# Gain rows spread by 128-row products, squares ahead of the gain copies, two recurrence copies on ScalarE, and a new instruction order, in a two-block token mixer

## The chip, the cores and the metric

The kernel runs on one core of a Trainium2 chip. The metric is the time on the device of one execution in microseconds: the median of three runs.

## What is computed

The reference is two transformer-like blocks, one behind the other, on 1024 tokens of width 1024, in float32. The first is cut here to what the change touches:

```python
def rms_norm(x, g):
    y = x * lax.rsqrt(jnp.mean(x * x, axis=-1, keepdims=True) + NORM_EPS)
    return y * g

h = rms_norm(x, pre_norm_w)
p = h @ w_in                       # 8320 columns: recurrence, convolution, pooling, gates
p_rwkv = token_shift(p_rwkv, mu)   # p + (p_prev - p) * mu
# per head (8 heads of 64), over 1024 tokens:
sa = state @ a_t
state = state * w_t + outer(sa, b_t) + outer(v_t, k_t)
y_t = state @ r_t
# group norm, bonus and gate; convolution and pooling branches; three gated
# branch projections; output projection; residual
```

The second block has windowed attention with sinks, a retention in both directions, and a feed-forward part of 2816 hidden channels whose last product is the down projection.

## The kernel before

All large products are float32 by parts: each operand is split into a high part, rounded for TensorE (`Whi`, `Hhi`), and the rest (`Wlo`, `Hlo`), and three products hi x hi, lo x hi and hi x lo are summed in PSUM (`dense`). ScalarE makes the high part, VectorE or GpSimd the low one. The first product is written in quarters of 256 tokens for its first two 128-column tiles, since the normed tokens are not all there yet.

**The start.** The tokens come in 8 tiles of 128 (`xs`, 5 buffers). ScalarE squares and sums each (`token_squares`, into `xj`), GpSimd raises the sum to -1/2 (`rstd`, `ss`), VectorE multiplies tile, factor and gain row (`token_norms`, into `xn`, 3 buffers), TensorE transposes 128x128 pieces into PSUM (`tokens_in`), ScalarE rounds them into `Hhi` and VectorE makes `Hlo`. The gain row is needed on all 128 partitions: TensorE multiplies a column of ones, 1x128, by the row, 1x512 twice, and ScalarE copies the result to `g_row` (`begin`). `xn0` holds the ones and `xn1` the row until the first norms. `WARM` counts the products of zeros that TensorE runs before and behind this.

**The recurrence.** The scan is cut into chunks of 64 tokens. A unit is two heads by 512 tokens, 8 units in all, 8 chunks each. Per unit `prep` makes decays and keys (`Cc`, `Ee`, `kkn`, `rk`, `kp`, `BK`), `invert` builds the chunk matrices (`AB`) and inverts them on VectorE by 60 small steps (`Nn`, `Ntmp`), `stage` turns them into the chunk operators (`WU`, `Zt`), and `chain` carries the state `Xs` from chunk to chunk: a product on TensorE, a multiply on VectorE, 64 times. All of it is woven into the stream of dense products of the first projection (`kb`, `rb`, `RAV` are its results for keys, r and v). Two steps matter here: the copies of the transposed values from PSUM into `WU` rows 64 to 127 (VectorE, in `stage`, two per unit; ScalarE copies rows 0 to 63), and the transposition of the inverse inside SBUF into `Nt` (VectorE, last step of `invert`; the trace calls both `Nn`), which SP then writes out (`scr_xt`).

**The down projection.** A Strassen-like scheme with 7 block products (`PRODUCTS["w"]`). Its weights come as `wSrcA..`, VectorE sums them to `wSrcS..`, ScalarE rounds to `wHi..`, VectorE or GpSimd make `wLo..`; the hidden values (`hT..`, `hB..`) go the same way, and the results are summed in `acc`.

**What sets the order.** Each engine's program is a set of streams (generators), one letter each, and `weave` takes steps from them in the order of a string per engine in `ORDER`. The engines run strictly in that order, and synchronize by semaphores alone. `PICKS` says which PSUM bank each use takes. In `ORDER["pe"]` d is a dense step (two 512-column products), a a token transposition, p, i, s, c and g are the recurrence's streams; in `ORDER["act"]` Z is `begin`, q the squares, a the rounding of tokens, w the weight rounding.

The helpers record all operations at one line each: products L120, transposes L123, ScalarE L126, VectorE's and GpSimd's two-operand operations L129, scalar ones L133 and L134, with a tensor L137, copies L140, memsets L143, transfers L146.

## Time and profile before

| | |
|---|---|
| runs | 2243.98, 2244.04, 2244.3 us; median 2244.04 |
| the profiled execution | 2244.64 us |
| its span, first to last instruction | 2242.9 us |
| busy: PE, VectorE (DVE), ScalarE (ACT), GpSimd (POOL) | 99%, 69%, 37%, 21% |
| mean granted clock of TensorE | 0.998 |

A share of busy time is read against the span. The busy time of PE includes products that run at a lower clock, and a product's record is longer than the time to the next one's start, since products are pipelined: how fast they run is read from the distance of their starts. A row's idle time stands in brackets with what ended it.

### The profile page before, as it was taken

Reading aid. Unit: us, or ns where it says so; the run is one execution under the profiler, and the core shown is the slowest. Engines: PE = TensorE matmul, PEld = TensorE weight load, DVE = VectorE, ACT = ScalarE, POOL = GpSimd, SP = SyncE. Lnnn points to the kernel's source line nnn. Section 1 sums busy time; section 2 is a strip of 40 time slices with the busy share of each in tenths; the row PEclk is TensorE's granted clock in tenths of the full one; section 3 lists DMA queues with packets and bytes.
Section 4 is the critical chain, followed back from the end, with each engine's and each line's share of the span. In section 5 each row is a group of like instructions: output and inputs, shape, how many; then the busy total and the mean of one; then the engine's idle time right before and its main releaser. Section 6 shows DMA issues by size and latency. Waiting matters only on the chain.

```text
span 2242.9 us, 30930 instructions
## 1 busy us (share of the span) xinstructions
PE 2218.5 (99%) x11960; PEld 1835.1 (82%) x11960; DVE 1554.3 (69%) x2646; ACT 837.8 (37%) x1486; POOL 476.1 (21%) x379
## 2 busy tenths in 40 slices
PE   9999999999999999999999999999999999999998
PEld 7778788777788888888888888888888888887777
DVE  6775886778858444665448777754776666678998
ACT  5334243333444334223334454542333333345441
POOL 2000000000002321143122212200122222236552
PEclk9999999999999999999999999999999999999999
DMA  4122221221233334853221212133222222233334
GB/s 151 44 57 53 64 58 35 62 56 58 65 113 116 113 113 150 291 169 129 91 72 52 59 38 59 39 127 113 76 85 85 85 78 82 85 115 106 107 122 149
DMA packets 254547, 208.55 MB, mean 93 GB/s; under 512 B 49985, under 2 KB 223681, under 8 KB 254402
## 3 DMA queue, kind: packets, MB, share of 16 engines
q1 hardware_dynamic: 254400, 206.58, 29.6%
q8 instruction: 95, 1.56, 0.3%
q14 instruction: 50, 0.41, 0.1%
q10 hardware_dynamic: 2, 0.00, 0.0%
HBM read 151.48 MB, written 47.71 MB: 89 GB/s over the span
## 4 chain that ended last, share of the span: by engine, by line
PE 79%; DVE 14%; issue 2%; DMA 2%; SPq 1%; POOL 1%; ACT 1%; DVEq 0%; POOLq 0%; ACTq 0%
PE PS L120 77%; PE PS L123 3%; DVE Nn L129 2%; DVE Ntmp L129 2%; SPq L146 1%; DVE Wlo L129 1%; DMA Nn<-scr_ns 1%; DVE acc L129 1%; DMA wSrcA<-in_w_down_dram 1%; DVE wSrcS L129 1%; DVE Zt L129 1%; DVE cy L137 1%; DVE ST L137 1%; POOL wLoA L129 0%; DVE Xs L129 0%
## 5 line engine op out<-in xcount | busy, mean ns | idle before, releaser
L120 PE MATMUL PS<-Hhi,Wlo 128*128 128x512 f32 (+1 forms) x1304 | 421.4, 390 | 0.0
L120 PE MATMUL PS<-Hlo,Whi 128*128 128x512 f32 (+1 forms) x1304 | 420.5, 389 | 0.0
L120 PE MATMUL PS<-Hhi,Whi 128*128 128x512 f32 (+1 forms) x1304 | 419.5, 388 | 0.9 <-DVE Hlo L129 0.9
L120 PEld LDWEIGHTS PS<-Hhi,Whi 128*128 128x128 f32 x1304 | 240.3, 189 | 45.9 <-issue 2.0
L120 PEld LDWEIGHTS PS<-Hhi,Wlo 128*128 128x128 f32 x1304 | 239.1, 189 | 45.9 <-issue 2.4
L120 PEld LDWEIGHTS PS<-Hlo,Whi 128*128 128x128 f32 x1304 | 239.6, 189 | 44.9 <-issue 2.2
L126 ACT ACTIVATE Whi<-Wraw 128x512 fp32r<-128x512 f32 x170 | 106.4, 629 | 333.7 <-PE PS L120 333.3
L129 DVE TENSOR_TENSOR Wlo<-Wraw,Whi 128x512 fp32r<-128x512 f32 x166 | 121.4, 734 | 73.2 <-ACT Whi L126 72.4
L129 DVE TENSOR_TENSOR Ntmp<-Nn 32x30 f32<-32x30 f32 (+14 forms) x240 | 76.7, 319 | 23.3 <-DMA Nn<-scr_ns 17.1
L129 POOL TENSOR_TENSOR sm<-sm,expo 128x8 f32<-128x8 f32 x8 | 17.3, 2165 | 340.4 <-DVE sm L134 340.3
L129 DVE TENSOR_TENSOR Nn<-Nn,Ntmp 32x30 f32<-32x30 f32 (+14 forms) x240 | 76.6, 319 | 6.9
L129 DVE TENSOR_TENSOR acc<-PS,acc 128x512 f32<-128x512 f32 x108 | 71.0, 679 | 10.4 <-PE PS L120 10.2
L129 POOL TENSOR_TENSOR Wlo<-wA,Whi 128x512 fp32r<-128x512 f32 x38 | 51.0, 1342 | 110.6 <-ACT Whi L126 110.6
L129 DVE TENSOR_TENSOR wS<-wA,wA 128x512 f32<-128x512 f32 x38 | 26.1, 688 | 57.9 <-DMA wA<-in_w_gate_dram 57.9
L120 PE MATMUL PS<-YMlo,Whi 128*128 128x512 f32 (+1 forms) x188 | 64.7, 372 | 0.0
L120 PE MATMUL PS<-YMhi,Whi 128*128 128x512 f32 (+1 forms) x188 | 64.6, 371 | 0.0
L120 PE MATMUL PS<-YMhi,Wlo 128*128 128x512 f32 (+1 forms) x188 | 64.5, 371 | 0.0
L126 ACT ACTIVATE smx<-smx,small,q_norms 128x385 f32<-128x385 f32 (+1 forms) x64 | 43.1, 675 | 47.7 <-DVE small L137 47.7
L129 POOL TENSOR_TENSOR rsb<-rsb,expo 128x8 f32<-128x8 f32 x8 | 13.2, 1654 | 218.3 <-DVE rsb L133 218.3
L120 PE MATMUL PS<-YMhi,fSlo 128*128 128x512 f32 x152 | 59.1, 389 | 0.0
L120 PE MATMUL PS<-YMlo,fShi 128*128 128x512 f32 x152 | 59.1, 389 | 0.0
L120 PE MATMUL PS<-YMhi,fShi 128*128 128x512 f32 x152 | 59.1, 389 | 0.0
(497 smaller groups left out, 5216.8 us busy)
## 6 DMA issues: line engine op xcount, KB each, us to landing
Wraw<-in_w_in_dram SPq DMA_DIRECT2D x126, 256.0 KB, 2.9
scr_g<-stg SPq DMA_DIRECT2D x24, 512.0 KB, 3.1
tg<-scr_g SPq DMA_DIRECT2D x24, 512.0 KB, 4.3
scr_fb<-fb SPq DMA_DIRECT2D x22, 512.0 KB, 4.1
gwA<-in_w_in_dram SPq DMA_DIRECT2D x40, 256.0 KB, 3.4
wA<-in_w_gate_dram SPq DMA_DIRECT2D x38, 256.0 KB, 3.2
wA<-in_w_up_dram SPq DMA_DIRECT2D x38, 256.0 KB, 3.3
wSrcA<-in_w_down_dram SPq DMA_DIRECT2D x48, 192.0 KB, 2.9
```

What stands on the lines that cost most here:

```text
L120: return self.h.matmul(out, lhsT, rhs, start=start, stop=stop, skip_group_check=True)
L123: return self.h.transpose(out, in_, ident)
L126: return self.h.activation(out, in_, func, **kw)
L129: return self.h.tensor_tensor(out, a, b, op)
L137: return self.h.scalar_tensor_tensor(out, a, s, b, op0, op1)
L146: return self.h.dma_start(out, in_)
```

## The change

Six things change.

1. The gain row is spread by products with 128 rows: `xn2` columns 0 to 127 are zero but for row 0, which is 32, and `xn1` is zero but for row 0, the gains. VectorE fills `xn2`, GpSimd fills all of `xn1` first, and the transfer of the row, on ScalarE's queue, waits for that. The factor 32 was in ScalarE's copy before.
2. `WARM` goes from (4, 8) to (5, 2).
3. ScalarE squares the first three token tiles ahead of the gain copies, which now wait for the norm of tile 1.
4. VectorE norms tiles 0 and 1 with the gains read from PSUM, and from tile 2 on with `g_row`.
5. ScalarE copies both halves of `WU` and makes the `Nt` transposition.
6. All five order strings and the bank picks are new.

```diff
--- before.py
+++ after.py
@@ -17,7 +17,7 @@
 ORDER2 = ("aq", "rk", "rv", "rq")
 NXS, NXN = 5, 3
 NRAW, NSPL = 3, 4
-WARM = (4, 8)
+WARM = (5, 2)
 KAPPA = float(np.exp(-0.5))
 EPS = 1e-6
 GN_EPS = 64 * 1e-5
@@ -659,11 +659,11 @@
         pe.wait_ge(*S.start_dve.at("zero"))
         for i in range(WARM[0]):
             pe.mm(SB[3], K.Whi[NSPL - 1][:, 0, :], K.Whi[NSPL - 1][:])
+        pe.wait_ge(*S.start_dve.at("one"))
         pe.wait_ge(*S.grow_dma.at(0))
         for j in range(2):
-            bank, _ = banks.take(("gain", j), (f"SB{j}",), [S.init_act.at("gain")])
-            t = pe.mm(bank, K.xn[0][0:1, 0:128], K.xn[1][0:1, j * 512:j * 512 + 512])
-        t.then_inc(*S.xtr_pe.tick("gain"))
+            bank, _ = banks.take(("gain", j), (f"SB{j}",), [S.init_act.at("gain"), S.xn_dve.at((1, j))])
+            pe.mm(bank, K.xn[2][:, 0:128], K.xn[1][:, j * 512:j * 512 + 512]).then_inc(*S.xtr_pe.tick(("gain", j)))
         for i in range(WARM[1]):
             t = pe.mm(SB[3], K.Whi[NSPL - 1][:, 0, :], K.Whi[NSPL - 1][:])
         t.then_inc(*S.xtr_pe.tick("warm"))
@@ -949,7 +949,7 @@
             cb = hf * 8
             na = K.NA[u % 2]
             for g in range(2):
-                bk, before = banks.take(("av", u, g), SIDE, [S.stage_act.at(("a", u, g)), S.stage_dve.at(("v", u, g))])
+                bk, before = banks.take(("av", u, g), SIDE, [S.stage_act.at(("a", u, g))])
                 for m in before:
                     pe.wait_ge(*m)
                 pe.wait_ge(*S.prep_dve.at(("r", u)))
@@ -977,7 +977,7 @@
             for m in before:
                 pe.wait_ge(*m)
             pe.wait_ge(*S.inv_dve.at(("A", u, 1, 1)))
-            pe.wait_ge(*S.stage_dve.at(("v", u, 1)))
+            pe.wait_ge(*S.stage_act.at(("a", u, 1)))
             for c in range(8):
                 for h in range(2):
                     t = pe.mm(bk[64 * h:64 * h + 64, c * 64:(c + 1) * 64], na[64:128, h, c, :], K.WU[64:128, h, c, 64:128])
@@ -1253,11 +1253,13 @@
         return (S.w_raw0, S.w_raw1, S.w_raw2)[n % NRAW].at(n)
 
     def begin():
+        act.wait_ge(*S.xrstd_pool.at("row"))
         act.dma(K.xn[1][0:1, :], K.D["pre_norm_w"]).then_inc(*S.grow_dma.tick(0, by=16))
         yield
-        act.wait_ge(*S.xtr_pe.at("gain"))
+        act.wait_ge(*S.xtr_pe.at(("gain", 1)))
+        act.wait_ge(*S.xn_dve.at((1, 1)))
         for j in range(2):
-            act.act(K.g_row[:, j * 512:j * 512 + 512], banks.of(("gain", j)), ACT.Copy, scale=32.0).then_inc(*S.init_act.tick("gain"))
+            act.act(K.g_row[:, j * 512:j * 512 + 512], banks.of(("gain", j)), ACT.Copy).then_inc(*S.init_act.tick("gain"))
         yield
 
     def weights():
@@ -1411,12 +1413,18 @@
                 src = banks.of(("av", u, g)).rearrange("p (c h f) -> p h c f", c=4, h=2)
                 act.wait_ge(*S.stage_pe.at(("av", u, g)))
                 act.wait_ge(*S.init_dve.at("wu"))
-                act.act(K.WU[0:64, :, 4 * g:4 * g + 4, 0:64], src[0:64], ACT.Copy).then_inc(*S.stage_act.tick(("a", u, g)))
+                act.act(K.WU[0:64, :, 4 * g:4 * g + 4, 0:64], src[0:64], ACT.Copy).then_inc(*S.stage_act.tick())
+                act.act(K.WU[64:128, :, 4 * g:4 * g + 4, 64:128], src[64:128], ACT.Copy).then_inc(*S.stage_act.tick(("a", u, g)))
                 yield
                 src = banks.of(("bk", u, g)).rearrange("p (c h f) -> p h c f", c=4, h=2)
                 act.wait_ge(*S.stage_pe.at(("bk", u, g)))
                 act.act(K.BKT[:, :, 4 * g:4 * g + 4, :], src, ACT.Copy).then_inc(*S.stage_act.tick(("bk", u, g)))
                 yield
+            act.wait_ge(*S.inv_dve.at(("dg", u)))
+            if u:
+                act.wait_ge(*S.xtw_dma.at(u - 1))
+            act.act(K.Nt, K.Nn[0:16].rearrange("p s t -> p t s"), ACT.Copy).then_inc(*S.stage_act.tick(("nt", u)))
+            yield
             act.wait_ge(*S.stage_pe.at(("m1", u)))
             act.wait_ge(*S.init_dve.at("v1"))
             for a in range(0, 128, 32):
@@ -1823,9 +1831,11 @@
     omu, bones, maskA, rst = K.omu, K.c_("bones"), K.c_("maskA"), K.c_("rst")
 
     def begin():
-        dve.memset(K.xn[0][0:1, 0:128], 1.0).then_inc(*S.start_dve.tick("one"))
         dve.memset(K.xse[:, :, 1024:1025], float(np.sqrt(1024 * EPS))).then_inc(*S.start_dve.tick("eps"))
         dve.memset(K.Whi[NSPL - 1][:].bitcast(F32), 0.0).then_inc(*S.start_dve.tick("zero"))
+        dve.memset(K.xn[2][:, 0:128], 0.0).then_inc(*S.start_dve.tick("rows"))
+        dve.wait_ge(*S.start_dve.at("rows"))
+        dve.memset(K.xn[2][0:1, 0:128], 32.0).then_inc(*S.start_dve.tick("one"))
         dve.memset(K.expo[:], -0.5).then_inc(*S.start_dve.tick("expo"))
         yield
 
@@ -1839,13 +1849,17 @@
                 yield
 
     def token_norms():
-        dve.wait_ge(*S.init_act.at("gain"))
         for i in range(8):
+            if i == 2:
+                dve.wait_ge(*S.init_act.at("gain"))
             if i >= NXN:
                 dve.wait_ge(*S.xtr_pe.at((i - NXN, 1)))
             dve.wait_ge(*S.xrstd_pool.at(i))
             for cols, keys in ((slice(0, 512), [(i, 0)]), (slice(512, 1024), [(i, 1), i])) if i < 2 else ((slice(0, 1024), [(i, 0), (i, 1), i]),):
-                dve.stt(K.xn[i % NXN][:, cols], K.xs[i % NXS][:, cols], K.ss[:, 8 + i:9 + i], K.g_row[:, cols], ALU.mult,
+                gain = banks.of(("gain", keys[0][1])) if i < 2 else K.g_row[:]
+                if i < 2:
+                    dve.wait_ge(*S.xtr_pe.at(("gain", keys[0][1])))
+                dve.stt(K.xn[i % NXN][:, cols], K.xs[i % NXS][:, cols], K.ss[:, 8 + i:9 + i], gain, ALU.mult,
                         ALU.mult).then_inc(*S.xn_dve.tick(*keys))
                 yield
 
@@ -2057,11 +2071,6 @@
             dve.wait_ge(*S.inv_dve.last())
             dve.ts(dg, dg, 1.0, ALU.add).then_inc(*S.inv_dve.tick(("dg", u)))
             yield
-            if u:
-                dve.wait_ge(*S.xtw_dma.at(u - 1))
-            dve.wait_ge(*S.inv_dve.last())
-            dve.cp(K.Nt, Nn[0:16].rearrange("p s t -> p t s")).then_inc(*S.inv_dve.tick(("nt", u)))
-            yield
 
     def stage():
         for u, (p, hf) in enumerate(UNITS):
@@ -2072,13 +2081,6 @@
             dve.cp(EC[:, 0, :], K.Ee[0:64, :, 64]).then_inc(*S.stage_dve.tick())
             dve.cp(EC[:, 1, :], K.Ee[64:128, :, 64]).then_inc(*S.stage_dve.tick(("EC", u)))
             yield
-            for g in range(2):
-                src = banks.of(("av", u, g)).rearrange("p (c h f) -> p h c f", c=4, h=2)
-                dve.wait_ge(*S.stage_pe.at(("av", u, g)))
-                if u:
-                    dve.wait_ge(*S.stage_pe.at(("de", u - 1, 1, 1)))
-                dve.cp(K.WU[64:128, :, 4 * g:4 * g + 4, 64:128], src[64:128]).then_inc(*S.stage_dve.tick(("v", u, g)))
-                yield
             for g in range(2):
                 for h in range(2):
                     b3 = banks.of(("de", u, g, h))[0:64, :].rearrange("p (i j x f) -> p i j x f", i=2, j=2, x=2)
@@ -2680,6 +2682,8 @@
         pool.tt(out, out, K.expo[:, 0:out.shape[1]], ALU.pow).then_inc(*sig.tick(key))
 
     def token_norms():
+        pool.memset(K.xn[1][:], 0.0).then_inc(*S.xrstd_pool.tick("row"))
+        yield
         for i in range(8):
             pool.wait_ge(*S.start_dve.at("expo"))
             pool.wait_ge(*S.xsq_act.at(i))
@@ -2869,7 +2873,7 @@
             sp.wait_ge(*S.inv_dve.at(("dg", u)))
             sp.dma(D["scr_xs"][u], K.Nn.rearrange("p s t -> p (s t)")).then_inc(*S.xsw_dma.tick(u, by=16))
             yield
-            sp.wait_ge(*S.inv_dve.at(("nt", u)))
+            sp.wait_ge(*S.stage_act.at(("nt", u)))
             sp.dma(D["scr_xt"][u], K.Nt.rearrange("p s t -> p (s t)")).then_inc(*S.xtw_dma.tick(u, by=16))
             yield
             xs_v = D["scr_xs"][u].rearrange("(b q) (s t) -> b s q t", b=2, s=32)
@@ -3164,68 +3168,68 @@
 
 ORDER = {
     "pe":
-        "a5d24a2d14a2d36a2d7a2d27a2d10a2d78pd5pd8pd18id3pd20id7s2d5s2d4pd5pd9pd19id41pd5id7s2d4sd7s2d5s2d5scs"
...
+        "a4d18a3d17a2d22a2d8a2d20a2d10ad2ad99pd4pd8pd20id3pd19sdsd3s2d5id4pd4pd8pd16id61pd4id9s2d4sd5s2d3s2d3"
...
```

Three places of the order. First ScalarE at the start of the program, as a piece of the difference (`xj` are the squares, `g_row` the gain copies; - before, + now):

```order
-L126 ACTIVATE g_row<-PS 128x512 x2
 L126 ACTIVATE xj,ss<-xs 128x1025 x2
-L126 ACTIVATE Hhi<-PS 128x4x128
 L126 ACTIVATE Whi_55<-Wraw_52 128x512
-L126 ACTIVATE Whi_56<-Wraw_53 128x512
-L126 ACTIVATE Hhi<-PS 128x4x128
 L126 ACTIVATE xj,ss<-xs 128x1025
 L126 ACTIVATE Hhi<-PS 128x4x128
+L126 ACTIVATE Whi_56<-Wraw_53 128x512
+L126 ACTIVATE Hhi<-PS 128x4x128
+L126 ACTIVATE g_row<-PS 128x512 x2
 L126 ACTIVATE xj,ss<-xs 128x1025
```

The gain copies moved from the first place to behind the third square and the second `Hhi`; the second `Whi` moved behind the first `Hhi`.

Second, VectorE at the end of the fourth inversion and the shift of the third `kb`, before:

```order
L133 TENSOR_SCALAR Nn<-Nn 32x32
L2132 TENSOR_REDUCE sm<-Yy 128x8
L129 TENSOR_TENSOR Wlo_62<-Wraw_53,Whi_58 128x512
L134 TENSOR_SCALAR sm<-sm 128x8
L140 COPY Nn<-Nn 16x1024
L137 SCALAR_TENSOR_TENSOR kb<-PS,par,kb 128x1023
```

and now:

```order
L133 TENSOR_SCALAR Nn<-Nn 32x32
L129 TENSOR_TENSOR Yy<-Yy,BV_92 128x512
L129 TENSOR_TENSOR Wlo_62<-Wraw_53,Whi_58 128x512
L137 SCALAR_TENSOR_TENSOR kb<-PS,par,kb 128x1023
```

The first row ends the inversion. The transposition is gone from between it and `kb`. On ScalarE, at the same place, now (`rk` is the square of `kb` that TensorE waits for):

```order
L126 ACTIVATE Nn_95<-Nn_95 16x1024
L126 ACTIVATE Whi3_58<-Wraw1_53 128x512
L126 ACTIVATE kb_81<-PS,drv_65 128x1024
L126 ACTIVATE rk_89<-kb_81,par_64 128x512
```

where before the rows were the same without the first.

Third, ScalarE in the down projection, between the third and the fourth weight block of 384 columns, before:

```order
L126 ACTIVATE hB21hi3_318<-hB21raw3_320 128x512
L126 ACTIVATE acc10_356<-PS 128x512
L126 ACTIVATE acc12_358<-PS 128x512
L126 ACTIVATE wHiS3_326<-wSrcS3_344 128x384
L126 ACTIVATE acc19_365<-PS 128x512
L126 ACTIVATE hT4hi3_321<-hT21_281 128x512
L126 ACTIVATE acc18_364<-PS 128x512
L126 ACTIVATE hB11hi0_236<-hB11raw0_238 128x512
L126 ACTIVATE wHiS4_328<-wSrcS4_345 128x384
```

and now:

```order
L126 ACTIVATE hB21hi3_318<-hB21raw3_320 128x512
L126 ACTIVATE acc10_356<-PS 128x512
L126 ACTIVATE wHiS3_326<-wSrcS3_344 128x384
L126 ACTIVATE acc12_358<-PS 128x512
L126 ACTIVATE acc19_365<-PS 128x512
L126 ACTIVATE wHiS4_328<-wSrcS4_345 128x384
```

`hT4hi3`, `acc18` and `hB11hi0` moved behind the weights.

## Rows read from the trace of the kernel before

**Rows 1.** The page: busy time, share of the span and instructions of each engine.

```profile
PE 2218.5 (99%) x11960; PEld 1835.1 (82%) x11960; DVE 1554.3 (69%) x2646; ACT 837.8 (37%) x1486; POOL 476.1 (21%) x379
```

**Rows 2.** Who waited for whom, PE: total us, times, longest.

```profile
PE PS L120 <- DVE Xs L129: 2.5, 6, 0.7
PE PS L120 <- ACT rk L126: 2.2, 3, 1.1
PE PS L120 <- ACT wHiS L126: 2.1, 2, 1.9
PE PS L120 <- DVE wLoS L129: 2.0, 5, 0.6
```

**Rows 3.** Windows: stretch, length, PE, PEld, DVE, ACT, POOL busy, granted clock, DMA, GB/s.

```profile
324.50:327.90 3.40, 3.40 (x9) 2.63 (x8) 0.05 (x1) 0.35 (x1) 2.25 (x2) 0.50 0.48 106
2051.70:2055.10 3.40, 3.40 (x10) 2.64 (x9) 1.44 (x2) 1.31 (x4) 3.27 (x3) 0.50 0.23 66
```

**Rows 4.** Timeline, 2048 to 2056: start us, duration us, engine, operation [idle before, releaser].

```profile
2048.99 0.60 ACT L126 ACTIVATE acc<-PS 128x512 f32<-128x512 f32 x1 [0.74 <-PE PS L120]
2049.62 0.63 ACT L126 ACTIVATE hB11hi<-hB11raw 128x512 fp32r<-128x512 f32 x1
...
2048.09 1.53 DVE L129 TENSOR_TENSOR wSrcS<-wSrcA,wSrcS 128x384 f32<-128x384 f32 x1
...
2050.80 0.47 PE L120 MATMUL PS<-hB22hi,wHiS 128*128 128x512 f32 x1 [1.85 <-ACT wHiS L126]
...
2052.46 0.63 PE L120 MATMUL PS<-hB22hi,wLoS 128*128 128x512 f32 x1
2052.89 0.63 PE L120 MATMUL PS<-hB22hi,wHiS 128*128 128x512 f32 x1
...
2055.53 0.40 PE L120 MATMUL PS<-hT2lo,wHiS 128*128 128x512 f32 x1
2055.76 0.39 PE L120 MATMUL PS<-hT2hi,wLoS 128*128 128x512 f32 x1
```

**Rows 5.** Timeline of the start, and the landing times of the token tiles (tile xs).

```profile
3.58 3.78 PE L120 MATMUL PS<-xn,xn 1*128 1x512 f32 x4
...
7.29 3.58 PE L120 MATMUL PS<-Whi 128*128 128x512 f32 x8
7.39 1.08 ACT L126 ACTIVATE g_row<-PS 128x512 f32<-128x512 f32 x2 [4.85 <-PE PS L120]
8.36 1.06 ACT L126 ACTIVATE xj<-xs 128x1025 f32<-128x1025 f32 x1
...
11.25 0.63 PE L123 MATMUL PS<-cst,xn 128*128 128x128 f32 x4 [0.38 <-DVE xn L137]
...
14.91 0.36 PE L120 MATMUL PS<-Hhi,Whi 128*128 128x256 f32 x1 [0.89 <-DVE Hlo L129]
...
18.80 0.36 PE L120 MATMUL PS<-Hhi,Whi 128*128 128x256 f32 x1
...
DMA to landing us min/median/max: 3.6/5.8/8.0
```

**Rows 6.** Groups by line and form, GpSimd's copies and VectorE's largest memset: busy, mean ns.

```profile
L140 POOL COPY kp<-rsb 128x512 f32<-128x512 f32 x8 | 5.6, 696 | 0.4
...
L143 DVE MEMSET WU<- 64x1024 f32 x1 | 0.9, 912 | 0.3 <-issue 0.3
```

**Rows 7.** Timeline, 321.9 to 323.

```profile
321.99 0.72 ACT L126 ACTIVATE rk<-kb,par 128x512 f32<-128x512 f32 x1 [2.45 <-DVE kb L137]
...
322.86 1.02 PE L120 MATMUL PS<-cst,rk 128*128 128x2 f32 x8 [1.06 <-ACT rk L126]
```

**Rows 8.** Groups by line and form, the copies that move, and ScalarE's into WU.

```profile
L140 DVE COPY WU<-PS 64x512 f32<-64x512 f32 x16 | 11.1, 694 | 5.2 <-PE PS L123 4.8
L140 DVE COPY Nn<-Nn 16x1024 f32<-16x1024 f32 x8 | 8.9, 1107 | 0.7
...
L126 ACT ACTIVATE WU<-PS 64x512 f32<-64x512 f32 x64 | 37.9, 592 | 34.1 <-PE PS L120 17.3 <-PE PS L123 15.9
```

More of the change, by code:

```diff
@@ L3227 @@
[L3227 to L3228 removed]
+    "2320101320132013200101011010010101011010011001010101010101001010110100101111010101010100101011010011"
+    "0101010101001010101101010110101011010101001101010010101101010101010010101010110100101111010101010100"
+    "1010010110101010100100101010101010101101010010101011067423501674235016742350167423501674235016742350"
@@ new lines @@
+    "1671010101010101010101010102102010110101001201101010120012011012012012012001201201201102102201200120"
+    "1021012101201210210210200120120120112012012010201021101201201021022120120002012012011201201200120120"
+    "1201210121021020120120102012010210211021021021012012010201021101201201012001011010120100110120101245"
+    "0123674501236745012367450123674501236745012367450123674501236745012367450123674501236745012360174560"
+    "1237456012374560123745602137456021374560213745602137456021374123012134231022137502201020321"
```

102 lines of the change are left out of this document (47 added, 55 removed).

## The prediction, made before the change ran

> **What bounds the kernel now.** I read the engine shares first, then who waited for whom on TensorE, then the timeline at the longest waits. [rows 1]: PE is busy 2218.5 us of the 2242.9 us span, every other engine 69% or less. So a change can gain only what PE loses: idle time, or time on a slow clock. Idle is 2242.9 - 2218.5 = 24.4 us, 1.1% of the span. [rows 2] names it: PE waited 2.5 us for Xs (the recurrence's state), 2.2 us for rk, 2.1 us for wHiS, 2.0 us for wLoS, and less for the rest. The second loss is not in the busy time. In two stretches of 3.4 us the granted clock was 0.50 [rows 3], that is 1.2 instead of 2.4 GHz. In the second of them 512-column products follow each other every 0.43 us, right behind it every 0.23 us [rows 4]: 3.41/0.43 = 8 products where 15 would fit, so one such stretch costs (0.43 - 0.23) x 8 = 1.6 us. Both come right behind a wait of PE: 1.06 us for rk at 322.9 [rows 7], 1.85 us for wHiS at 2050.8 [rows 4].
>
> The profiled execution took 2244.64 us (span 2242.9), 0.6 us over the median 2244.04. The sum is made against 2244.64, and 0.6 comes off at the end.
>
> **The start: -2.0 us.** Before, ScalarE has nothing to do until the gains are spread. PE runs 4 warm products, waits for the row, runs the four records of the 1-row products in 3.78 us and the 8 warm products in 3.58 us, 0.45 each, near the 0.43 of [rows 4] at half the clock: this was 1.2 GHz too. ScalarE copies the gains at 7.39 (1.08 us) and only then squares, from 8.36, though the first token tile landed 3.6 us after its issue at 0.72, at 4.3 [rows 5]. The first transposes run at 11.25 and the first dense product at 14.91 [rows 5].
>
> What now happens, step by step. (1) GpSimd fills xn1, 128x1024, before the row's transfer may start. The trace has no such fill. Bounds: 0 us and 1.4 us, two of its 128x512 copies of 0.70 [rows 6]; VectorE's 64x1024 memset took 0.91 [rows 6], nearest in shape, and GpSimd is the slower of the two elsewhere, so I take 1.1. The row then leaves at about 1.9 instead of 0.71. It landed at most 2.9 us after its issue (3.58 - 0.71); now it goes beside the token tiles, so I take 3.1: it lands at 5.0. (2) PE: 5 warm products end at 1.6 + 5 x 0.43 = 3.7, PE waits 1.3 us, the gain products take 3.4 us (four records, 0.85 apart) to 8.4, two warm products to 9.3. The first transposes come at 9.3 instead of 11.25. (3) ScalarE squares tiles 0 and 1 from 4.3, 1.06 and a 0.2 us read each, to 6.9, and is free of the gains. Its next square waits for tile 2, which leaves SP ahead of one 256 KB weight piece now: median landing 5.8 us behind issue at 3.87 was 9.7, now some 0.8 earlier, 8.8. Then square 2 to 10.0, Hhi 0.60, Whi 0.62, Hhi 0.60 to 11.9; Hlo on VectorE 0.69 and hand-overs 0.3: first dense product at 12.9, 2.0 earlier. (4) VectorE reads the gains of tiles 0 and 1 from PSUM: its copies out of PSUM took 0.69 us for 512 columns [rows 8], no more than the 0.75 of this product from SBUF, so I count 0. (5) The second half of the contraction needed Hlo of (1,1), and began at 18.80. Now behind 11.9: gain copies 1.1, square 1.25, Hhi 0.6, Whi 0.6, Hhi 0.6, Hlo 0.9 = 17.0. Again about -2.0. The later tiles are then fed by ScalarE, which began its squares 4 us earlier, so nothing should take the 2 us back. Bounds: -3.4 (the row lands unhindered, the clock rises during the gain products, which saves half of their 3.4 us) and +1.7 (below). Five warm products fewer are inside this count.
>
> **The recurrence copies: -1.2 us.** Per unit VectorE loses two WU copies, 2 x 0.694, and the Nn transposition, 1.107: 2.5 us, over 8 units 20 us. ScalarE takes the first two at 2 x 0.592 [rows 8] and the third at about what VectorE needed: 2.3 us per unit, 18 us. It has room (37% busy, [rows 1]), and PE does not wait for either engine's total. What counts is the 2.5 + 2.2 = 4.7 us that PE waited for Xs and rk, both behind VectorE [rows 2]. Only one of these waits shows a moved copy in its chain, the one at 322.9: rk waited 2.45 us for kb, and PE then 1.06 us for rk [rows 7]; the Nn copy stood right ahead of kb on VectorE (the second place of the order). Now ScalarE has the Nn copy ahead of its own kb copy, with one Whi between them, where before it made the kb copy while VectorE transposed. Counted from the end of the inversion the chain to rk gets no shorter, so this wait goes only if the inversion ends earlier. It may: VectorE has 2.5 us less to do per unit. I take a quarter of the 4.7 us, -1.2. Bounds: all of it, -4.7, and as much again, +4.7, since every step of the order moved and each new place can be late. The slow stretch at 324.5 I leave in: 0, with bounds of -1.6 and, for a third one, +1.6.
>
> **The new order in the down projection: -3.3 us.** At 2048.6 PE waits 1.85 us for wHiS. The operand wSrcS is computed by 2049.6, but ScalarE works in order and has an acc copy that waits 0.74 us for PE, and hB11hi, ahead of wHiS [rows 4]. The third place of the order shows this wHiS right behind acc19, and on VectorE its source now stands ahead of hT1lo and hT, two subtractions that stood ahead of it. With hB11hi (started 0.5 us before wHiS could) and the late acc out of the way, and the source two 512-column subtractions of 0.6 to 0.7 us earlier, 1.7 of the 1.85 us go, and with the wait the slow stretch behind it, 1.6 us. Bounds: 0 (another operand is as late) and -3.5. The shorter wLoS waits, 2.0 us in five [rows 2], stay: 0. The last 30 rows of PE stand as before: 0.
>
> **Sum**: 2244.64 - 2.0 - 1.2 - 3.3 = 2238.1; less 0.6 is 2237.5 us, -0.3%.
>
> **A rule against the change.** The first 256-column dense products, from 14.91, ran 0.12 us apart, the pace of 2.4 GHz, although 16 transposes were all that PE did in the 3.6 us ahead of them. The Trainium skill (TensorE: Matmul & The Clock Gate, Part 4) says that a transpose does not count as busy time for the clock the way a product does, and Part 1 that the clock is slow until PE has been kept busy. By that rule the wait for the row and two warm products instead of eight leave the clock low at 12.9. What it would cost is rival C; the trace so far speaks for the clock staying up, since the same transposes did it no harm.
>
> **The rivals.**
> A (forecast), 2237.5: start, copies and the down projection as above. For it: each of the three has a row. Chance 0.50, its own range 2234 to 2241.
> B, the order gives it back: the start gains 2.0, but new waits and a new slow stretch take the place of the old ones, as nearly every row moved and the old order too left 24.4 us idle. 2244.0 - 2.0 + (0 to 2) = about 2242.5. Chance 0.25.
> C, the slow clock at the first dense products: PE idles 1.3 us in the middle of its warm-up, and the clock is still at 1.2 GHz, or falls to it, for one stretch like those of [rows 3] from 12.9 on. That costs 1.6 us, and the rest comes as in A: 2239.1. Against it: before, 3.58 us of warm products went ahead of the transposes; now 3.4 + 0.9 = 4.3 us of 128-row products do. Chance 0.08.
> D, slower: ScalarE reaches the Nn transposition before the inversion ends and stands there, with the weight conversions (Whi) of the dense stream behind it. VectorE cannot make Wlo, and PE starves. One converted piece feeds PE for 24 products of 0.23 = 5.5 us, so this begins to cost when ScalarE stands longer than that; 1.3 us over it per unit is 8 x 1.3 = 10.4, less the 5.3 of the start and the down projection: 2244.0 + 5.1 = 2249.1. Against it: ScalarE is idle 63% of the span, so it can run several pieces ahead. Chance 0.08.
> E, more goes: the slow stretch at 324.5 too, and all but 1.2 of the 4.7 us for Xs and rk: 2237.5 - 1.6 - 2.3 = 2233.6. Chance 0.09.
>
> **How the numbers follow.** A measurement tells 0.2%, 4.5 us, from no change: the borders are 2239.6 and 2248.5. Faster: 0.42 of A's 0.50, E's 0.09, 0.05 of C, 0.02 of B: 0.58. Slower: D beyond the border, 0.07. Same: 0.35. The range leaves out D and the lower part of E: 2232.5 to 2244.5.
>
> **What would show it.** In the new profile: the first square at about 4.3, first transposes near 9.3, first dense product near 12.9 at 0.12 us spacing. Spacing 0.21 there means C. No wait for wHiS at 2046 and clock 1.00 around it. PE's waits for Xs and rk under 4.7 us in sum. Nn on ScalarE with idle time before it, followed by PE waits for Whi or Wlo, would mean D. The prediction is wrong if PE's idle time is 24 us again, or if the slow stretches are two or more.

## The result, and the profile after

| | before | after |
|---|---|---|
| median of the runs timed together, us | 2244.16 (20 runs) | 2247.93 (20 runs) |
| ratio, 95% interval | | 1.0018, 1.0011 to 1.0025 |
| profiled execution, us | 2244.64 | 2249.11 |
| its span, us | 2242.9 | 2247.0 |

The changed kernel is slower by 3.8 us, a difference just inside the 0.2% that I called no change and well outside my range (2232.5 to 2244.5). It was forecast faster by 6.5 us. Both signs that I had named for a wrong prediction are there: PE's idle time is over 24 us, and the slow stretches are two.

First the groups that answer to [rows 1] and [rows 2], of the changed kernel: the page's shares, then who waited for whom on PE.

```profile
PE 2217.8 (99%) x11955; PEld 1834.4 (82%) x11955; DVE 1534.7 (68%) x2623; ACT 864.8 (38%) x1510; POOL 487.0 (22%) x380
```

```profile
PE PS L120 <- DVE wLoS L129: 3.7, 7, 1.6
PE PS L120 <- ACT wHiS L126: 3.5, 3, 1.4
PE PS L123 <- DVE smx L133: 2.5, 2, 2.0
PE PS L120 <- DMA xn<-in_pre_norm_w_dram: 1.5, 1, 1.5
```

PE is as busy as before and idles 29.2 us instead of 24.4. Xs and rk have left the head of the list; wLoS and wHiS have grown from 4.1 to 7.2 us, and a wait for smx is new.

To see where, I cut both spans at the same dense products. The windows of the kernel before are the start, the recurrence, the plain stretch, attention with retention, the feed-forward, and the down projection with the end (columns as in [rows 3]):

```profile
0.00:14.90 14.90, 11.45 (x32) 6.53 (x33) 4.72 (x10) 7.54 (x13) 3.21 (x8) 1.00 0.59 198
14.90:715.90 701.00, 692.36 (x4104) 569.76 (x4104) 536.83 (x1089) 262.45 (x463) 54.52 (x38) 1.00 0.24 67
715.90:1171.00 455.10, 454.32 (x2105) 379.25 (x2104) 235.81 (x265) 154.76 (x240) 114.91 (x87) 1.00 0.43 142
1171.00:1515.00 344.00, 342.89 (x2473) 287.30 (x2472) 256.08 (x582) 166.46 (x326) 74.20 (x58) 1.00 0.22 63
1515.00:2020.00 505.00, 504.21 (x2302) 419.73 (x2301) 322.20 (x395) 159.43 (x268) 120.34 (x104) 1.00 0.28 90
2020.00:2242.90 222.90, 213.30 (x951) 172.54 (x949) 198.70 (x306) 87.12 (x179) 108.94 (x85) 0.98 0.39 119
```

and those of the changed kernel:

```profile
0.00:13.80 13.80, 9.28 (x24) 5.30 (x24) 4.97 (x11) 7.58 (x13) 5.07 (x10) 1.00 0.85 293
13.80:707.90 694.10, 689.99 (x4107) 569.46 (x4108) 510.27 (x1065) 289.99 (x486) 59.55 (x37) 1.00 0.24 67
707.90:1163.10 455.20, 454.42 (x2106) 379.15 (x2105) 236.02 (x266) 154.72 (x240) 116.09 (x88) 1.00 0.43 142
1163.10:1513.40 350.30, 345.84 (x2473) 288.41 (x2472) 254.07 (x581) 166.06 (x326) 75.72 (x58) 1.00 0.22 61
1513.40:2018.40 505.00, 504.22 (x2302) 419.75 (x2301) 320.98 (x396) 159.74 (x269) 123.42 (x104) 1.00 0.28 90
2018.40:2247.00 228.60, 214.09 (x951) 172.35 (x949) 208.38 (x305) 86.73 (x179) 107.12 (x86) 0.98 0.38 117
```

The first number behind each stretch is its length. Start -1.1 us, recurrence -6.9, attention +6.3, down projection with the end +5.7; the other two stretches are equal to 0.1 us. In the two stages whose code it edits the change gains 8 us, where I had 3.2. It loses 12 us in two stages where it alters nothing but the order and the choice of PSUM banks.

These shares come from one trace of each kernel. Seven of the traces below, this one and those of runs 1, 3, 4, 8, 10 and 11, share the changed start, copies and order of the recurrence; at the plain stretch they lead the trace of the kernel before by 5.3 to 9.5 us, this one by 7.9. So a stage's figure from one pair of traces may be off by some 2 us, and the ratios of whole runs carry the argument.

The slow clock moved too. In the changed kernel the granted clock is 0.50 from 1195.7 and from 2066.1:

```profile
1195.70:1199.10 3.40, 3.40 (x10) 2.64 (x9) 3.27 (x8) 0.56 (x1) 0.15 (x1) 0.50 0.20 52
2066.10:2069.50 3.40, 2.96 (x7) 2.39 (x8) 3.07 (x3) 0.73 (x2) 3.40 (x3) 0.50 0.04 11
```

The stretch at 324.5 [rows 3] is gone, one in the attention has come, and in the down projection the place is 2066.1 instead of 2051.7. The first begins 1.5 us behind the end of PE's longest wait of its stage, 2.02 us for smx at 1194.2. The second begins at 2066.1, inside the longest wait of its stage, 1.55 us for wLoS, which ends at 2066.5; the wait before that one, 1.42 us for wHiS, ends at 2064.3.

### The profile page after: what moved, and what is told of

The parts are those of the page before. It is cut to its first block, busy times and chain, and to the rows that moved or that the text cites. A ratio compares the mean times of both kernels' runs of the same rounds, so it can differ in the third digit from the quotient of the medians.

```text
span 2247.0 us, 30905 instructions
## 1 busy us (share of the span) xinstructions
PE 2217.8 (99%) x11955; PEld 1834.4 (82%) x11955; DVE 1534.7 (68%) x2623; ACT 864.8 (38%) x1510; POOL 487.0 (22%) x380
## 4 chain that ended last, share of the span: by engine, by line
PE 80%; DVE 13%; DMA 2%; issue 2%; ACT 1%; POOL 1%; SPq 1%; DVEq 0%; ACTq 0%; POOLq 0%
PE PS L120 77%; PE PS L123 3%; DVE Ntmp L129 2%; DVE Nn L129 2%; DMA wSrcA<-in_w_down_dram 1%; DVE wSrcS L129 1%; DVE ST L137 1%; SPq L146 1%; DVE acc L129 1%; DVE Wlo L129 1%; DVE wLoS L129 1%; DVE Zt L129 0%; DVE Xs L129 0%; DVE hT L129 0%; POOL wLoA L129 0%
## 5 line engine op out<-in xcount | busy, mean ns | idle before, releaser
L126 ACT ACTIVATE WU<-PS 64x512 f32<-64x512 f32 x80 | 47.4, 593 | 36.5 <-PE PS L123 18.0
L129 POOL TENSOR_TENSOR wLoA<-wSrcA,wHiA 128x384 fp32r<-128x384 f32 (+1 forms) x48 | 54.1, 1145 | 11.9 <-ACT wHiA L126 11.9
```

The source lines that it names most:

```text
L126: return self.h.activation(out, in_, func, **kw)
L129: return self.h.tensor_tensor(out, a, b, op)
```

## The experiments

All ratios are against the kernel before, timed in alternation with each; 0.001 is 2.2 us. The recurrence and the attention are separated by a plain stretch that takes the same time in both traces (455.1 and 455.2 us), and so are the attention and the down projection by the feed-forward (505.0 in both). In the middle of these one order can be cut off and the other set on.

**1 to 4. Which stage loses?** Each kernel takes the order and the banks of each stage from one of the two kernels.

```diff
 ORDER, PICKS              recurrence   attention   down projection
 early_new                 changed     -changed     -changed
                                       +before      +before
 late_new                 -changed      changed      changed
                          +before
 down_old                  changed      changed     -changed
                                                    +before
 attention_old             changed     -changed      changed
                                       +before
```

The start goes with the recurrence.

> The changed kernel up to the middle of the plain stretch of dense products after the recurrence (all edits of the code, its order of the start and the recurrence), and from there on the order and banks of the kernel before. Theory 1 (each stage keeps what its own order gives: start and recurrence -7.9 us, attention and retention +6.3, down projection +5.0, read at the same dense products of the two traces): about 7.9 us under the kernel before, 2236.3, a ratio of 0.9965. Theory 2 (the later losses come from the earlier part being 8 us early, by another timing of transfers and of the clock, whatever the order of the later stages): the loss is here too, 2244 to 2248. Theory 3 (the gain up to the middle is real, but any change of timing costs a slow stretch of the clock or two): 2238 to 2241.

> The reverse: the kernel before with its own code and order up to the same place, and from there on the changed kernel's order and banks (attention, retention, feed-forward, down projection). Theory 1: +6.3 and +5.0, about 2255.5, a ratio of 1.005. Theory 2: no loss, 2243 to 2246. Theory 3: 2246 to 2250.

> The changed kernel with the order and banks of the kernel before from the middle of the feed-forward stretch on, so in the down projection alone. Theory 1: the changed kernel less 5.0 us, 2242.6, 1.6 us under the kernel before. Theory 2: as the changed kernel, 2247 to 2248, since what comes ahead is the same. In the trace the waits of TensorE for wHiS and wLoS near 2062 us should be gone by theory 1.

> The changed kernel with the order and banks of the kernel before in the attention and retention stage alone (from the middle of the plain stretch to the middle of the feed-forward). Theory 1: the changed kernel less 6.3 us, 2241.3, and no wait of 2 us for smx near 1192 us nor the slow clock behind it. Theory 2: 2247 to 2248.

| | ratio, 95% | theory 1 |
|---|---|---|
| early_new | 0.9966, 0.9953 to 0.9978 | 0.9965 |
| late_new | 1.0056, 1.0043 to 1.0068 | 1.005 |
| down_old | 0.9986, 0.9977 to 0.9995 | 0.9993 |
| attention_old | 0.9995, 0.9986 to 1.0004 | 0.9987 |

Theory 1 holds in all four, theory 2 in none. Every order carries its gain or loss with it, whichever half stands ahead: 0.9966 and 1.0056 leave +0.0022 together, and the change measured +0.0018. So the later stages do not lose because they begin 8 us earlier; they lose because of how their own steps stand. Order and PSUM banks were always exchanged together here, so the four runs don't tell one from the other. Theory 3, slow stretches brought by any change of timing, was the rival in runs 1 and 2. It is not in the medians, but the one trace of run 1 has two slow stretches, from 14.2 and from 1423.9.

**5. The start alone.** The changed start, and everything behind it as before.

> The kernel before with the changed start alone (row products with 128 rows, memsets, warming products 5 and 2, first two tiles normed from PSUM, and the order of the first 13 us); everything behind the first few dense products, the recurrence's copies too, as before. My sum had -2.0 us; the trace of the changed kernel has the first dense product only 1.1 us earlier. Theory 1 (the stages add up): 1.1 us under the kernel before, ratio 0.9995. Theory 2 (an early shift is used up by the next wait for data): no change, 1.000.

Measured 0.9987, 0.9978 to 0.9996: 2.9 us, more than either theory. In its trace the first dense product is 1.3 us earlier, and the lead grows to 1.7 us by 297 us and to 2.9 by 368 us. Between these two lies 324.5, where the kernel before had its slow stretch and this run had none. Theory 2 is refuted. The slow stretch is missing in run 9 too, whose start is the old one and whose wait for rk at 321.7 is longer (1.49 us against 1.06), so its absence does not need the changed start; 1.3 us is what this trace gives to the start itself.

**6 and 9. The copies with the old order.** Before's order and start, with the 16 WU copies and the 8 Nn copies on ScalarE. First the Nn copy stood right before the step that reads m1:

```diff
 ScalarE, each unit
     bk(1)
-    m1
+    Nt <- Nn
+    m1
```

> The kernel before with its own order and start, but with the copies of the recurrence moved: the 16 copies into the second half of WU and the 8 transposing copies of Nn run on ScalarE, each at the place in ScalarE's order where its result is next read there (the Nn copy right before the step that reads m1). Theory A (the copies themselves bring the recurrence's gain, by taking some 20 us of work off VectorE): most of the 6.8 us, 2238 to 2240. Theory B (they bring it only together with the new order, which uses the freed time): within 1.5 us of the kernel before, 2242.5 to 2245. Theory C (my rival D: ScalarE stands at the Nn copy before the inversion ends, and its queue is late for what TensorE reads): slower, 2247 or more.

It took 2321.08 us, 1.0342: slower as in theory C, and far beyond it, but by another way, since ScalarE never stood at the copy; it came to it late. The waits of PE in its trace:

```profile
PE PS L120 <- DMA X11t<-scr_xt: 54.7, 8, 9.4
```

The copy goes to DRAM and comes back transposed before PE can use it. Counted from the copy's begin on ScalarE to the step on m1 this took 8.6 to 9.9 us in each of the eight units. The inversion ended at 346.8 in the fourth unit, and ScalarE began the copy only at 359.5. The 54.7 us are not the whole of the 77. The stretch of the recurrence, which ran from 14.9 to 715.9 in the kernel before, is now

```profile
15.00:793.00 778.00, 718.76 (x4103) 592.41 (x4104) 517.29 (x1066) 289.56 (x487) 53.51 (x38) 0.94 0.21 61
```

PE idles 59.2 us in it instead of 8.6, and is busy 26.4 us longer with the same products, since the granted clock is 0.50 in eight stretches of it, 95.6 us in all; seven of them are 10 to 20 us long. So the place is what failed, and I put it where ScalarE stood in the trace of before when the inversion ended:

```diff
 ScalarE, each unit
     bk(1)
+    Nt <- Nn
     (2 to 9 steps of other streams)
-    Nt <- Nn
     m1
```

(The 32 places and the 4 us in the text below are slips of mine: it is 2 to 9 places, and the copies had begun 6.2 to 14.4 us behind the inversion's end.)

> As the run with the copies alone, but the eight transposing copies of Nn stand in ScalarE's order where, in the trace of the kernel before, the inversion ends (ScalarE's next instruction there starts 0.3 us or more after VectorE's step on the diagonal), 2 to 32 places ahead of where they stood. In that run each began 4 to 15 us after the inversion's end, and TensorE waited 54.7 us for X11t, the transfer behind it. Theory C' (only the place of the Nn copy cost it): those waits go, and the time is within 3 us of the kernel before, 2241 to 2247. Theory C'' (ScalarE is late all through the recurrence with 20 us more work in this order): still over 2255.

Measured 0.9991, 0.9982 to 1.0000: theory C'. The same instructions on the same engine cost 77 us or gain 2, the latter at the edge of the interval, by the place of eight of the 24 copies alone. The wait for X11t is gone from its list; the one for Xs is down to 0.8, but rk now costs more than in [rows 2]:

```profile
PE PS L120 <- ACT rk L126: 2.9, 3, 1.5
...
PE PS L120 <- DVE AB L129: 1.8, 2, 1.2
```

**7 and 13. The recurrence without the start; its order without the copies.**

> The start of the kernel before, then the changed kernel's copies and its order of the recurrence, then the order of the kernel before from the middle of the plain stretch on. Theory 1: the 6.8 us that the traces show between the first dense product and 700 us, 2237.3, a ratio of 0.997; with the start alone it must add up to the -7.9 of the kernel with both. Theory 2 (start and recurrence work on one another): only -4 or less.

Measured 0.9968, 0.9956 to 0.9981: theory 1. The two parts add up to -0.0045 by their ratios, where the kernel with both has -0.0034; the intervals allow that. Then the copies went back to VectorE, in the new order:

```diff
 VectorE, each unit
     EC
+    WU[64:128] <- av(0)      (where ScalarE's copy began)
+    WU[64:128] <- av(1)
 ...
     Nn diagonal
+    Nt <- Nn
```

> The changed start and the changed order of the recurrence, but the copies on VectorE as in the kernel before: each WU copy stands in VectorE's order where ScalarE's began in the changed kernel's trace, the Nn copy right behind the inversion; from the middle of the plain stretch on as before. With the copies too this kernel was at a ratio of 0.9966, and with the start alone at 0.9987, so order and copies together bring 0.0021, some 5 us. Theory K (the copies bring it, the order only follows): 0.9985 to 0.999, as with the start alone. Theory L (the order brings it, whoever copies): 0.9966 to 0.9972. Theory M (this order has no room for 20 us more of VectorE): above 1.000.

Measured 1.0012, 1.0003 to 1.0021: theory M. The waits of PE in its trace:

```profile
PE PS L120 <- DVE Xs L129: 6.9, 15, 0.8
PE PS L120 <- DVE AB L129: 3.4, 4, 1.3
```

against these of the kernel with copies and order (the seventh run):

```profile
PE PS L120 <- DVE RAV L129: 1.5, 3, 0.7
...
PE PS L120 <- DVE Xs L129: 1.0, 4, 0.4
```

With the start's share (0.9987) taken off, the recurrence reads: copies with the old order -0.0009, order without the copies +0.0025, both -0.0021 to -0.0032. Neither part brings the gain by itself as it was tried. That the new order has no room for 20 us more on VectorE is my reading and is not shown: the copies stood at one set of places only, and runs 6 and 9 show how much a place can do.

**8. Two steps exchanged in the attention.** At 1191 PE stands for smx. All engines of the changed kernel there:

```profile
1191.12 0.49 DVE L137 SCALAR_TENSOR_TENSOR ST<-ST,small,PS 64x64 f32<-64x64 f32 x2
...
1191.51 2.35 POOL L129 TENSOR_TENSOR ro<-ro,sinT 128x1024 f32<-128x1024 f32 x1 [20.85 <-DMA ro<-qr]
...
1191.65 2.43 DVE L133 TENSOR_SCALAR smx<-smx,small 128x384 f32<-128x384 f32 x1
1194.11 0.49 DVE L137 SCALAR_TENSOR_TENSOR ST<-ST,small 64x64 f32<-64x64 f32 x2
...
1194.22 0.85 PE L123 MATMUL PS<-cst,smx 128*128 128x128 f32 x6 [2.02 <-DVE smx L133]
```

VectorE's scaling took 2.43 us; the median of this instruction is 0.41. It began 0.14 us behind GpSimd's product and ended 0.22 us behind its end. The exchange puts it 0.49 us earlier:

```diff
 VectorE
     small <- 1/small
+    smx <- smx*small
     ST <- ST*small+PS  (2)
-    smx <- smx*small
     ST <- ST*small     (2)
```

> The changed kernel with two neighbouring steps of VectorE exchanged, near 1191 us: the scaling of smx that TensorE waits 2.0 us for now stands ahead of two additions into ST that nobody waits for. In the changed kernel it began at 1191.65, 0.14 us behind GpSimd's product of 128x1024 (1191.51 to 1193.86), and ended at 1194.08, 2.43 us for what takes 0.41 elsewhere. Theory P (a VectorE operation with two operands or such a scaling stands while GpSimd's runs, so the place decides who pays): smx takes 0.4 us, TensorE's wait of 2.18 us goes, the slow clock of 3.4 us at half speed behind it (1.6 us) goes too, and the additions into ST take 2.4 us instead: 3.5 us under the changed kernel, 2244.2. Theory Q (the wait is for something else that is late, and only moves): less than 1 us.

The trace of that kernel:

```profile
1192.57 0.42 DVE L133 TENSOR_SCALAR smx<-smx,small 128x384 f32<-128x384 f32 x1
...
1193.15 2.39 POOL L129 TENSOR_TENSOR ro<-ro,sinT 128x1024 f32<-128x1024 f32 x1 [22.06 <-DMA ro<-qr]
1193.43 2.40 DVE L137 SCALAR_TENSOR_TENSOR ST<-ST,small 64x64 f32<-64x64 f32 x2
1193.57 0.88 PE L123 MATMUL PS<-cst,smx 128*128 128x128 f32 x6
```

and, as a window, the time in which the slow stretch had been:

```profile
1193.80:1200.00 6.20, 6.20 (x39) 5.04 (x39) 6.07 (x8) 1.12 (x2) 1.74 (x1) 1.00 0.07 17
```

Theory P in each point: smx takes 0.42 us, the two additions into ST take 2.40 instead of 0.49, PE doesn't wait, and the clock stays at 1.00. Across this place the trace gains 3.3 us on the changed kernel's. The ratio is 1.0005 (0.9996 to 1.0014) where the changed kernel had 1.0018 (1.0011 to 1.0025), 2.9 us less, and the two intervals overlap a little. The kernel before meets the same GpSimd product with additions into ST, which nobody reads soon.

Of these 3.3 us the wait is the exchange's, and the slow stretch may be chance. Runs 2, 3 and 10 have the old place of smx and waits of 2.1, 1.9 and 1.7 us for it; a slow stretch follows in run 3 alone. Against run 10, which had the wait and no slow stretch, the exchange gains 1.3 us at this place.

Not every instruction of VectorE stands. One that reads PSUM ran at its usual 0.55 us inside another such product of the changed kernel:

```profile
1365.98 2.39 POOL L129 TENSOR_TENSOR rot<-rot,sinT 128x1024 f32<-128x1024 f32 x1 [0.47 <-DMA rot<-ro]
...
1366.13 0.55 DVE L2319 CUSTOM_DVE_ANT_0 smx<-PS,cse 128x384 f32<-128x384 f32 x1
```

And where VectorE began first, at 1234.06 with a product of 128x1024 that took its usual 1.23 us, GpSimd's, begun at 1234.11, took 3.44 us instead of 2.39. The Trainium skill (SBUF — State Buffer, "SBUF: two separate sides") says that the two engines share a pair of ports, and that the instruction that starts first holds it to its end while the other stands; it says so of VectorE's instructions with two SBUF inputs, against a GpSimd instruction that reads SBUF, and of those in a two-port mode, not of all. The trace agrees: 2.43 us against 0.41 where GpSimd was first, 3.44 against 2.39 where VectorE was, and 0.55 as ever for the one that reads PSUM.

**10. One window of the down projection.** The first long waits there, in the changed kernel:

```profile
2062.37 0.68 DVE L129 TENSOR_TENSOR hT<-hB21raw,hT 128x512 f32<-128x512 f32 x1
2062.98 0.55 DVE L129 TENSOR_TENSOR wSrcS<-wSrcA,wSrcS 128x384 f32<-128x384 f32 x1
2063.09 0.63 ACT L126 ACTIVATE hT4hi<-hT 128x512 fp32r<-128x512 f32 x1 [2.76 <-DVE hT L129]
...
2063.63 1.33 ACT L126 ACTIVATE wHiS<-wSrcS 128x384 fp32r<-128x384 f32 x3
...
2065.13 2.63 DVE L129 TENSOR_TENSOR wLoS<-wSrcS,wHiS 128x384 fp32r<-128x384 f32 x2
```

```profile
2064.28 0.47 PE L120 MATMUL PS<-hB22hi,wHiS 128*128 128x512 f32 x1 [1.42 <-ACT wHiS L126]
...
2066.54 0.79 PE L120 MATMUL PS<-hB22hi,wLoS 128*128 128x512 f32 x1 [1.55 <-DVE wLoS L129]
```

On VectorE the source of S4's wHiS (the second row) stands behind hT and an acc addition, both of which it led in the old order. ScalarE stands 2.76 us at hT4hi with the three wHiS behind it. The edit gives this one window of 16 the old order:

```diff
 VectorE, fifth window            ScalarE, fifth window
-  hT3lo S3 hT2lo hT1lo loS3       -  ... B21hi hiS3 hT4hi hiS4 hiS2 hiS1 hiA12 hiA22
-  S1 acc S2 hT S4 acc             +  ... hiS3 acc acc B21hi hiS4 hiS2 hiS1 hiA12 hiA22 hT4hi
-  hT4lo loS4 loS2
+  S3 acc hT3lo loS3 S1 hT2lo S2
+  hT1lo S4 hT acc loS4 loS2
+  acc hT4lo
```

> The changed kernel with one of the 16 windows of the down projection (the fifth, 2054 to 2066 us) in the order of the kernel before: 18 steps of VectorE and 14 of ScalarE, so the sums S1, S2 and S4 stand ahead of two low halves and one addition into acc, and ScalarE's wHi copies ahead of hT4hi, for which it stood 2.76 us. Theory 1 (that order is what TensorE's waits of 1.59 and 1.72 us at 2062 and 2065 are from): they shrink to some 1.2 us together as in the run with the old down projection, and the slow clock at 2066.1 (1.6 us) goes; at most 2.1 + 1.6 us, so 2244 to 2246 against 2247.9. Theory 2 (the next window, in its new order, then waits for what this one did not): less than 1 us, 2247 to 2248.

Measured 1.0007, 0.9998 to 1.0016, 2.5 us under the changed kernel, whose interval (1.0011 to 1.0025) overlaps this one. The longest waits for wHiS and wLoS only fall from 1.42 and 1.55 to 1.0 and 1.1 us. The rest is the clock: this trace has no slow stretch in the down projection before its end. From 2020 us to the last dense product it gains 2.1 us on the changed kernel's, of the 5 that the whole stage lost. But runs 2 and 4 have this window in the new order with the same two waits, 1.4 and 1.6 us, and no slow stretch behind them either. So some 0.8 us of waits belong to this window; that the slow stretch does is not shown, and theory 2 is unlikely rather than refuted. The other windows were not tried one by one.

**11. The best of both in the down projection.** The changed order for its first four windows, where the trace had gained 3.0 us, and the old one behind.

> The changed start and recurrence; attention and retention as before; of the down projection the first four windows in the changed order and the rest as before. By the traces the changed order gains 3.0 us up to the fifth window (2061 against 2020 us) and loses 8 behind it. Theory 1: 3.0 under the kernel with all of the later order as before (ratio 0.9966), 2233, a ratio of 0.9953. Theory 2 (the wait of 2.2 us only moves to the fifth window): 2235.6 as without.

Measured 0.9971, 0.9959 to 0.9982: theory 2. The wait for wHiS, 2.05 us before 2046.0 in the trace of run 1, is gone, and three of 1.35, 0.74 and 1.09 us end at 2030.5, 2059.7 and 2061.5, with a slow stretch from 2062.1. It brings nothing over 0.9966 that could be told. The gain of my third term is given back within two windows.

**12 and 14. One row instead of 128.** The start waits for the row of norm weights. In the changed kernel:

```profile
0.71 0.95 POOL L143 MEMSET xn<- 128x1024 f32 x1 [0.29 <-POOLq L3318]
1.70 0.51 ACTq L146 DMA_DIRECT2D xn<-in_pre_norm_w_dram  x1
5.52 3.75 PE L120 MATMUL PS<-xn,xn 128*128 128x512 f32 x4 [1.55 <-DMA xn<-in_pre_norm_w_dram]
9.92 1.71 PE L123 MATMUL PS<-cst,xn 128*128 128x128 f32 x8
10.03 1.06 ACT L126 ACTIVATE xj<-xs 128x1025 f32<-128x1025 f32 x1 [0.73 <-DMA xs<-in_x_dram]
13.79 0.36 PE L120 MATMUL PS<-Hhi,Whi 128*128 128x256 f32 x1 [0.69 <-DVE Hlo L129]
```

```diff
-    pool.memset(K.xn[1][:], 0.0)
-    act.wait_ge(*S.xrstd_pool.at("row"))
-    dve.memset(K.xn[2][:, 0:128], 0.0)
-    pe.mm(bank, K.xn[2][:, 0:128], K.xn[1][:, j * 512:j * 512 + 512])
+    pe.mm(bank, K.xn[2][0:1, 0:128], K.xn[1][0:1, j * 512:j * 512 + 512])
```

> The kernel with the best of both orders, but with row products of one row as in the kernel before (no clearing of xn by GpSimd and VectorE, and the transfer of the norm weights does not wait for it), still read from PSUM and ahead of the copies. In the changed kernel the transfer is issued at 1.70 us, behind GpSimd's memset (0.71 to 1.66), TensorE stands 1.55 us for it and the row products begin at 5.52. Theory R (the clearing sets the start): the products begin some 0.9 us earlier and the first dense product at 12.9 instead of 13.8, 0.9 us less in all. Theory S (the slower clock or the transfers of x set it): within 0.2 us in the trace. Theory T (the products of 128 rows keep the clock up, and one row does not): the first dense products run at 0.24 us instead of 0.12 and 2 us are lost.

The trace of that run:

```profile
0.72 0.50 ACTq L146 DMA_DIRECT2D xn<-in_pre_norm_w_dram  x1
...
3.90 3.78 PE L120 MATMUL PS<-xn,xn 1*128 1x512 f32 x4
...
8.62 1.91 PE L123 MATMUL PS<-cst,xn 128*128 128x128 f32 x8
...
12.44 0.36 PE L120 MATMUL PS<-Hhi,Whi 128*128 128x256 f32 x1 [0.62 <-DVE Hlo L129]
```

Theory R: the row is there when the warming products end, the row products begin 1.6 us earlier, and the first dense product 1.15 us earlier than in the same kernel with 128 rows. The 1-row products take as long as those of 128 rows (3.78 and 3.75 us). The dense products follow at 0.12 us here, so theory T doesn't hold in this trace; it is taken up again below. The ratio was 0.9967 (0.9956 to 0.9978), against 0.9971 with 128 rows. Then the same edit on the kernel of run 1:

> The changed start and recurrence, everything behind as before (0.9966), with row products of one row and no clearing, as in the run that saved 1.15 us at the first dense product. If that stays until the end: 0.9961, 2235 against 2243.9 to 2244.7 of the kernel before; if the next wait uses it up: 0.9966.

Measured 0.9966, 0.9954 to 0.9979, equal to run 1. In its trace the 0.9 us of lead lasts from the first dense product to 1340 us; in the medians it can't be told. This trace has the first dense products at half speed, 0.21 us apart until 15.6 us:

```profile
13.73 0.41 PE L120 MATMUL PS<-Hlo,Whi 128*128 128x256 f32 x1
13.94 0.41 PE L120 MATMUL PS<-Hhi,Wlo 128*128 128x256 f32 x1
```

That is what theory T said of one row. But run 1, with 128 rows, has a slow stretch in the same place (last section), so two traces with one row neither show theory T nor refute it.

## Why the prediction was wrong, point by point

**The start, -2.0: measured -1.1.** The first square came at 4.24 as forecast (4.3). The step that failed is the row's landing: issued at 1.70 it took until 5.5, 3.8 us and not the 3.1 that I took, so the transposes came at 9.92, not 9.3. The square of tile 2 was forecast for 8.8 and came at 10.03, but runs 1, 5, 8 and 11 have it at 8.5 to 8.7, and their first dense product still at 13.6 to 13.8, so it is not what set the time. The first dense product came at 13.79, not 12.9. The nine traces with this start have it between 12.66 and 13.79, run 3 being the early one: its row landed as late, but its transposes ran from 9.30. So the gain is 1.1 to 2.3 us by the trace, and only run 3 reaches the forecast 2.0. The runs with one row show that the clearing of xn, priced right by itself (0.95 us for my 1.1), was on this path and bought nothing.

**The recurrence, -1.2: measured -6.9.** The waits for Xs and rk fell from 4.7 to 1.2 us, so 3.5 us went and not a quarter; all idle time of the stage fell from 8.6 to 4.1, and the slow stretch at 324.5, which I had left in at 1.6, did not come. These two make 6.1 of the 6.9. The step that failed is "a quarter of the 4.7": I traced one wait, saw that its chain gets no shorter, and sized the whole by it. Runs 7, 9 and 13 show the term belongs to copies and order together. ScalarE's price was wrong as well: it needs twice VectorE's 1.107 us for the transposing copy, so it takes on 27 us and not 18 (864.8 against 837.8), though no wait of PE in this stage hangs on it:

```profile
L126 ACT ACTIVATE Nn<-Nn 16x1024 f32<-16x1024 f32 x8 | 16.9, 2112 | 10.9 <-DVE Nn L133 10.8
```

**The down projection, -3.3: measured +5.0 to the last dense product.** The wait that I looked at went as forecast: at the dense product of 2061 us the changed kernel had gained 3.0 us over 2020 us, the wait of 1.85 us for wHiS gone and the slow stretch with it. But that stretch was chance and should have been counted in part. The old order has this wait in nine traces, 1.8 to 2.1 us each time; a slow stretch follows in five of them (the kernel before, runs 5, 7, 9 and 14) and in four not (runs 1, 3, 6 and 13). The step that failed is taking this window for the stage: it has 16 windows, all reordered, and "the shorter wLoS waits stay: 0" was an assumption without a row. Waits of 1.42, 1.55, 1.24, 0.81 and 1.09 us, the first two in the window right behind and the last at 2199, then took its place. The end behind the last dense product, which I had at 0, is 0.7 us longer.

**The missing term.** Attention and retention stood in no line of the sum, so at 0, and cost +6.3 us. I had counted edits of code; the order tables there were as new as elsewhere. Run 8 shows half of it, 3.3 us, in one pair of steps, slow stretch included. Behind it PE has waits of 0.3 to 0.7 us at five places, 2.4 us together, where the kernel before has 1.1 us at three; no run took these apart, and what is left of the 6.3 stays open.

**The rivals.** B, the order gives it back, came nearest: its mechanism is what happened, but I bounded what the new waits take beyond the start's gain at 2 us on the ground of old idle time, and it was 5.1 (6.3 + 5.7 - 6.9). D's first half occurred: ScalarE stood at the Nn copy for the inversion in five of the eight units, 1.1 to 3.6 us, and began it at most 0.8 us behind the inversion in all of them. That is under the 5.5 us from which I had said that it begins to cost, and PE waited for no Whi or Wlo of the projection in the recurrence. Run 6 shows a danger at the same copy that I had not priced, the transfer behind it. C did not occur in this trace, whose dense products follow at 0.12 us behind transposes with waits between them, so the cited rule on transposes did not decide it. E's lower waits came true inside a slower kernel.

**The sum by stages** is -1.1 - 6.9 + 6.3 + 5.7 = +4.0 against a span 4.1 us longer. Against the forecast the start is 0.9 us worse, the recurrence 5.7 better, the down projection with the end 9.0 worse and the attention 6.3 worse. So the down projection and the missing term are what turned the sign, and that the total is off by 10.4 us and not by 16 is luck in the recurrence. Nothing in the trace of before prices a new place among VectorE's 2623 instructions. What could have been done is a term with bounds of both signs for every reordered stage, as I gave the recurrence, and with it a wider range.

## What to carry to other kernels

Count a reordered stage as changed even when its code is not, and give it bounds of both signs; one window read closely says nothing of the fifteen others. Where two versions agree step by step for a stretch, splice them there: four runs told each stage's share, and the first of them, the changed start and recurrence with the rest as before, beats both kernels at 0.9966 (2235.6 us). On engines that work in order, ask of each step what it must not stand behind: 24 copies cost 77 us or gained 2 by the place of eight of them.

## What the runs showed of the hardware that I had not expected

A VectorE instruction from SBUF to SBUF that begins just behind a GpSimd product of 2.4 us stands for the rest of it (0.42 to 2.43 us for smx, 0.49 to 2.40 for the additions into ST), one that reads PSUM does not (0.55 us), and a GpSimd product that begins behind VectorE's is the one that stands (2.39 to 3.44 us). Beside GpSimd's powers of 128x8 elements VectorE does not stand: at 178.6 a subtraction of 128x512 took its usual 0.67 us inside one of 2.26 us. Who pays is decided by 0.49 us of order.

The clock's slow stretches are not fixed to a program or to a wait. The wait of 1.8 to 2.1 us for wHiS was followed by one in five of nine traces, that of 1.7 to 2.1 us for smx in two of four. Nine of the traced kernels have the changed start with 128 rows; in three of them, run 1 among them, the clock was 0.50 from 14.1 to 14.3 us on, at the first dense products, and in the others not:

```profile
14.20:17.60 3.40, 3.40 (x18) 3.40 (x17) 1.85 (x2) 1.89 (x4) 1.90 (x2) 0.50 0.95 323
```

With one row it is slow there in run 14 and not in run 12. So rival C does occur, in four of the eleven traces with the changed start and in none of the five with the old one, and a single trace must not be read for it. In run 1 it turned a lead of 1.2 us at the first dense product into a lag of 0.2 us by 17.6, near the 1.6 us priced. It also says how far a single trace may stand from its median: this one took 2239.44 us, its kernel's slowest, where the median is 2235.63.
